# Scores one item ahead, two-headed maps, all convolution taps on VectorE, and x tiles squared first

## What is computed

```python
def layer(x, mod, p, lam, rope, cache):            # per layer, context and latent tokens
    h = rms(x, norm1_g) * (1 + sc1) + sh1
    u = h @ w_in                                     # 1024 -> 2048, split among four mixers
    qa, ka, va, pool_in, glu_in, qd, kd, vd = split(u)
    o_a = softmax(rope(rms(qa)) @ rope(rms(ka)).T / 8) @ va       # 4 query heads, 2 key heads of 64
    o_b = multiscale_pool(pool_in)                   # windows 2, 4, 8, 16
    c = depthwise_conv(a * sigmoid(gate), conv_dw_w) + conv_dw_b  # 256 channels, 31 taps
    o_c = silu(layer_norm(c)) @ conv_pw_w
    # differential attention, 4 heads: q and k split into halves of 32
    P = softmax(q1 @ k1.T) - lam * softmax(q2 @ k2.T)
    o_d = rms(P @ vd, diff_subln_g) * (1 - lambda_init)
    x = x + g1 * concat(o_a, o_b, o_c, o_d) @ w_out
    h2 = rms(x, norm2_g) * (1 + sc2) + sh2
    return x + g2 * expert_choice_ffn(h2)            # 16 experts, SwiGLU, top-k tokens of each
```

## Time and profile before

| what | value |
|---|---|
| median of 3 runs | 2134.52 us (2133.85 to 2135.9) |
| profiled execution, its own time | 2133.39 us |
| its span, first to last instruction | 2131.6 us |
| TensorE clock granted, mean of the span | 0.93 of full |
| busy: PE, DVE, ACT, POOL | 1845.3, 591.4, 470.8, 449.6 us |
| phase 1, layer 0: x stage (to the first projection matmul), projections | to 59.4, to 232.8 us |
| phase 2, layer 0 | 232.8 to 396.9 us |
| experts, layer 0 (536 to 1068 us) | PE busy 525.6 of 532 us, DMA at 388 GB/s |
| phase 1, layer 1: first projection matmul | 1102.0 us |
| phase 2, layer 1: start | 1278.1 us |

### The profile page before, as it was taken

One profiled execution on the slowest core, in us unless ns is written; L12 is line 12 of the kernel. 1 busy time (PEld: TensorE's weight loads), 2 busy tenths in 40 slices (PEclk: granted clock), 3 DMA queues, 4 the chain that ended last, 5 costly groups with the idle time before them and its releaser, 6 DMA issues.

```text
span 2131.6 us, 38834 instructions
## 1 busy us (share of the span) xinstructions
PE 1845.3 (87%) x16748; PEld 920.7 (43%) x16748; DVE 591.4 (28%) x1035; ACT 470.8 (22%) x1208; POOL 449.6 (21%) x410
## 2 busy tenths in 40 slices
PE   3998677895999999999959878879849999999994
PEld 2554455452344444444435435544424444444442
DVE  1365455234011010110126644542331101101011
ACT  2100255111221221221220014441112212212122
POOL 0155233100111111111113642330001111111112
PEclk8999799896999999999969988999879999999997
DMA  9220700327799999999950125004339999999996
GB/s 384 88 79 0 300 36 1 139 89 279 278 401 394 395 401 395 394 402 395 401 219 1 79 98 238 1 1 178 148 108 381 402 394 395 401 394 402 394 394 240
DMA packets 146546, 539.16 MB, mean 253 GB/s; under 512 B 8304, under 2 KB 14544, under 8 KB 146480
## 3 DMA queue, kind: packets, MB, share of 16 engines
q1 hardware_dynamic: 118512, 468.88, 55.3%
q10 hardware_dynamic: 14400, 43.41, 5.4%
q0 software_dynamic: 13568, 25.96, 5.1%
HBM read 511.71 MB, written 26.64 MB: 253 GB/s over the span
## 4 chain that ended last, share of the span: by engine, by line
PE 66%; DMA 18%; DVE 5%; ACT 3%; issue 3%; SPq 1%; POOL 1%; POOLq 1%; ACTq 0%; DVEq 0%
PE PS L794 22%; DMA ring<-in_exp_w_up 15%; PE PS L802 11%; PE PS L723 7%; PE PS L527 4%; PE PS L486 4%; PE PS L487 3%; PE PS L586 2%; PE PS L488 2%; PE PS L425 2%; PE PS L666 2%; DMA ring<-in_w_mod 1%; PE PS L593 1%; SPq L369 1%; PE PS L639 1%
## 5 line engine op out<-in xcount | busy, mean ns | idle before, releaser
L794 PE MATMUL PS<-ring,arena 128*32 128x512 f32 x6144 | 684.6, 596 | 17.8 <-ACT gate_rows L902 9.2
L794 PEld LDWEIGHTS PS<-ring,arena 128*32 128x32 f32 x6144 | 202.0, 110 | 439.7 <-issue 406.5
L802 PE MATMUL PS<-ring,arena 128*32 128x256 f32 x6144 | 349.5, 379 | 0.0
L802 PEld LDWEIGHTS PS<-ring,arena 128*32 128x32 f32 x6144 | 205.5, 110 | 166.9 <-issue 56.7
L1694 POOL DMA_INDIRECT x_rows<-arena x64 | 102.2, 1597 | 652.8 <-DVE arena L1501 602.8
L1115 ACT ACTIVATE arena<-PS,modB,modA 128x64 f32<-128x64 f32 x272 | 84.0, 413 | 395.6 <-PE PS L781 395.6
L723 PE MATMUL PS<-ring,H 128*128 128x512 f32 x320 | 142.7, 606 | 1.2 <-DVEq L1173 1.2
L1680 POOL DMA_INDIRECT arena<-xn_rows,arena x68 | 68.0, 1000 | 343.2 <-DVE arena L1487 253.8
L1275 DVE SCALAR_TENSOR_TENSOR arena<-arena,par 128x655 f32<-128x655 f32 x106 | 121.9, 1150 | 3.5
L486 PE MATMUL PS<-ring,H 128*128 128x512 f32 x160 | 87.3, 629 | 22.1 <-DVE mod L1183 19.0
L1324 DVE TENSOR_REDUCE stat<-PS 128x2 f32<-128x1280 f32 (+1 forms) x60 | 76.6, 1277 | 107.4 <-PE PS L593 98.0
(11 more groups left out here) (209 smaller groups left out, 1937.7 us busy)
## 6 DMA issues: line engine op xcount, KB each, us to landing
ring<-in_exp_w_gate SPq DMA_DIRECT2D x64, 2048.0 KB, 17.8
ring<-in_exp_w_up SPq DMA_DIRECT2D x64, 2048.0 KB
ring<-in_exp_w_down SPq DMA_DIRECT2D x64, 2048.0 KB
ring<-in_w_mod SPq DMA_DIRECT2D x18, 2048.0 KB, 7.7
ring<-in_w_in SPq DMA_DIRECT2D x8, 2048.0 KB, 25.7
arena<-in_w_mod ACTq DMA_DIRECT2D x6, 2048.0 KB, 14.5
ring<-in_w_out SPq DMA_DIRECT2D x4, 2048.0 KB
arena<-x_rows ACTq DMA_DIRECT2D x15, 512.0 KB, 7.3
```

The costliest lines, as they stand in the source:

```text
L794: last = mm(PS[64 * c + r:64 * c + r + LANE, bank, :], left[:, c0 + r:c0 + r + LANE], ring[:, s0 + k // 4, k % 4, c * HALF:(c + 1) * HALF] ...
L802: last = mm(PS[32 * j:32 * j + 32, bank, 0:QUART], left[:, c0:c0 + 32], ring[:, s0 + k // 4, k % 4, j * QUART:(j + 1) * QUART], start=(k = ...
```

## The change

1. **Order on TensorE in the attention.** The body of the loop becomes `item(l, k)`. Item 0 comes first; then item k+1 is given out ahead of the pieces of item k.
2. **Order on ScalarE.** An item's exponentials come ahead of its pieces.
3. **Differential pairs.** A pair is now (c, part): for the two heads of chunk c the map of part 0 or of part 1. The scores are two matmuls of 512 columns on separate row groups and one of 256 for the cached keys (their host-side packing `spread` follows). The first pair of a unit isn't scaled, GpSimd scales the second (two instructions), and VectorE does both subtractions when the second pair is two back. gqa maps are scaled by two instructions instead of one.
4. **Taps.** All 62 are on VectorE: 18 after f(1), 31 after f(3), then 3, 3, 3, 4. GpSimd's taps, its buffer and the addition in item "mean" go; the last tap announces `c_y`.
5. **x stage.** ScalarE squares all five tiles before anything else, and VectorE normalises all five before its first evacuation. TensorE turns x(0) and x(1), does the first half of j(0), turns x(2) to x(4), does the second half of j(0), then f(0) to f(5). j(0) waits for the evacuation of tile 0 alone, f(0) for that of all.

```diff
-        PAIRS = (("gqa", 0), ("diff", 0), ("diff", 1), ("gqa", 1), ("diff", 2), ("diff", 3))
+        PAIRS = (("gqa", 0, 0), ("diff", 0, 0), ("diff", 0, 1), ("gqa", 1, 0), ("diff", 1, 0), ("diff", 1, 1))
...
+        def scaled(n):
+
+            return 4 * (n // 6) + (1, 1, 2, 3, 3, 4)[n % 6]
+
         def maps_of(v):
 
             t, kind, c, last = unit(v)
             bufs = probs if t < LT else probs_ctx
-            if kind == "gqa":
-                return [(bufs[last % 6], i * (TOK if t < LT else P)) for i in range(2)]
-            return [(bufs[(last - 1) % 6], 0), (bufs[last % 6], 0)]
+            buf = bufs[(last if kind == "gqa" else last - 1) % 6]
+            return [(buf, i * (TOK if t < LT else P)) for i in range(2)]
...
                     b0 = 2 + 3 * (t % 2)
                     if ks[0] == 0:
-                        pe.wait_ge(b0_evac, 10 * l + NT)
-                        pe.wait_ge(b1_evac, 10 * l + NT)
+                        pe.wait_ge(b0_evac, 10 * l + 1)
+                        pe.wait_ge(b1_evac, 10 * l + 1)
...
+                        if i == 0:
+                            pe.wait_ge(b0_evac, 10 * l + NT)
+                            pe.wait_ge(b1_evac, 10 * l + NT)
...
-                for t in range(NT):
+                step_x(l, 0)
+                step_x(l, 1)
+                step_j(l, 0, range(0, 4))
+                for t in range(2, NT):
                     step_x(l, t)
-                for ks in (range(0, 4), range(4, KD)):
-                    step_j(l, 0, ks)
-                    step_f(l, 0, ks)
-                for i in range(1, 6):
+                step_j(l, 0, range(4, KD))
+                for i in range(6):
...
-                    kind, i = PAIRS[r]
+                    kind, c, part = PAIRS[r]
                     area = set_at(k)
+                    qc, kc = (c, 2) if kind == "gqa" else (3 + c, 5 + c)
                     for m in range(2):
-                        if kind == "gqa":
-                            rows, qc, kc = slice(64 * m, 64 * m + 64), i, 2
+                        r0 = 64 * m + 32 * part
+                        rows = slice(r0, r0 + (64 if kind == "gqa" else 32))
+                        lhs = qkT[rows, qc, t * P:(t + 1) * P]
+                        if t < LT:
+                            mm(area[:, 1024 * m:1024 * m + LAT], lhs, qkT[rows, kc, 0:LAT], start=True, stop=True)
                         else:
-                            r0 = 32 * (2 * (i % 2) + m)
-                            rows, qc, kc = slice(r0, r0 + 32), 3 + i // 2, 5 + i // 2
-                        lhs = qkT[rows, qc, t * P:(t + 1) * P]
-                        if t == LT:
                             last = mm(area[:, 896 * m:896 * m + P], lhs, qkT[rows, kc, LAT:TOK], start=True, stop=True)
-                        elif m == 0:
-                            mm(area[:, P:512], lhs, qkT[rows, kc, 0:LAT - P], start=True, stop=True)
-                            left, right = lhs, qkT[rows, kc, LAT - P:LAT]
-                        else:
-                            mm(area[:, 1024:1536], lhs, qkT[rows, kc, 0:LAT], start=True, stop=True)
                     if t < LT:
-                        mm(area[:, 512:640], left, right, start=True, stop=True)
-                        for m in range(2):
-                            last = mm(area[:, 896 * m:896 * m + P], qkT[:, i if kind == "gqa" else 3 + i // 2,
-                                                                        t * P:(t + 1) * P],
-                                      kcS[:, 0 if kind == "gqa" else 1 + i, m * P:(m + 1) * P], start=True, stop=True)
+                        both = area[:, 512:1024].rearrange("p (a n) -> p a n", a=4)[:, 0:4:3, :]
+                        last = mm(both, qkT[:, qc, t * P:(t + 1) * P],
+                                  kcS[:, 0 if kind == "gqa" else 1 + 2 * c + part, :].rearrange("p (m n) -> p m n", m=2),
+                                  start=True, stop=True)
                     last.then_inc(t_scores, 1)
...
-                for k, (kind, x) in enumerate(ITEMS):
+                def item(l, k):
+                    kind, x = ITEMS[k]
...
+                item(l, 0)
+                for k in range(len(ITEMS)):
+                    if k + 1 < len(ITEMS):
+                        item(l, k + 1)
                     for v, piece in PIECES[k]:
...
+                for t in range(NT):
+                    squares(l, t)
...
-                squares(l, 0)
                 for t in range(NT):
-                    if t + 1 < NT:
-                        squares(l, t + 1)
...
-                    for v, which in PIECES[k]:
-                        piece(l, v, which)
                     if kind == "p":
                         exponentials(l, k, x)
...
+                    for v, which in PIECES[k]:
+                        piece(l, v, which)
...
+                    if (i, k) == (1, TAPS - 1):
+                        done.then_inc(c_y, 1)
+                    else:
+                        link(done)
+
+                taps = [(0, k) for k in range(TAPS)] + [(1, k) for k in range(TAPS)]
...
-                normalise(l, 0)
+                for t in range(NT):
+                    normalise(l, t)
...
-                conv_taps(16)
+                conv_taps(18)
                 step_f(l, 3)
-                conv_taps(20)
+                conv_taps(31)
...
-                    conv_taps(5 if t < LT else 4)
+                    conv_taps(3 if t < LT else 4)
...
-                    if PAIRS[r][0] == "gqa":
+                    if PAIRS[r][2] == 0:
                         return
                     w = TOK if t < LT else P
-                    out = (probs if t < LT else probs_ctx)[r]
+                    out = (probs if t < LT else probs_ctx)[r - 1]
+                    other = (probs if t < LT else probs_ctx)[r]
                     dve.wait_ge(t_rec, NP * l + n + 1)
-                    dve.wait_ge(p_scaled, NP * l + n + 1)
-                    V.scalar_tensor_tensor(out[:, 0:w], out[:, 0:w], stat[:, 80 + 2 * (n % 4):81 + 2 * (n % 4)],
-                                           out[:, w:2 * w], ALU.mult, ALU.add).then_inc(p_hat, 1)
+                    dve.wait_ge(p_scaled, NU * l + scaled(n))
+                    for m in range(2):
+                        c = 80 + 2 * ((n - 1) % 4) + m
+                        V.scalar_tensor_tensor(out[:, m * w:(m + 1) * w], out[:, m * w:(m + 1) * w], stat[:, c:c + 1],
+                                               other[:, m * w:(m + 1) * w], ALU.mult, ALU.add).then_inc(p_hat, 1)
...
-                        dve.wait_ge(c_part, l + 1)
-                        V.tensor_tensor(y3[:, 1, :], y3[:, 1, :], wb[:, 0:OUTW], ALU.add).then_inc(c_y, 1)
...
-                def conv_tap(k):
-                    if k == DVE_TAPS:
-                        return G.tensor_scalar(wb[:, 0:OUTW], u[:, 1, k:k + OUTW], cwT[:, 1, k:k + 1], None, ALU.mult)
-                    link(G.tensor_scalar(tap, u[:, 1, k:k + OUTW], cwT[:, 1, k:k + 1], None, ALU.mult))
-                    return G.tensor_tensor(wb[:, 0:OUTW], wb[:, 0:OUTW], tap, ALU.add)
...
+                        if PAIRS[r][0] == "diff" and PAIRS[r][2] == 0:
+                            continue
                         reach(t_rec, NP * l + x + 1)
-                        if PAIRS[r][0] == "gqa":
-                            both = out[:, 0:2 * w].rearrange("p (m n) -> p m n", m=2)
-                            G.tensor_tensor(both, both, rec.unsqueeze(2).to_broadcast([P, 2, w]),
-                                            ALU.mult).then_inc(p_scaled, 1)
-                        else:
-                            G.tensor_scalar(out[:, w:2 * w], out[:, w:2 * w], rec[:, 1:2], lams[:, 5:6],
-                                            ALU.mult, ALU.mult).then_inc(p_scaled, 1)
+                        for m in range(2):
+                            half_ = out[:, m * w:(m + 1) * w]
+                            if PAIRS[r][0] == "gqa":
+                                last = G.tensor_scalar(half_, half_, rec[:, m:m + 1], None, ALU.mult)
+                            else:
+                                last = G.tensor_scalar(half_, half_, rec[:, m:m + 1], lams[:, 5:6], ALU.mult, ALU.mult)
+                        last.then_inc(p_scaled, 1)
...
-                spread[l, r0:r0 + 32, 1 + h, m] = ckT[r0:r0 + 32, 1 + h // 2]
+                spread[l, r0:r0 + 32, 1 + 2 * (h // 2) + m, h % 2] = ckT[r0:r0 + 32, 1 + h // 2]
```

27 lines of the change are left out of this document (9 added, 18 removed).

## The result

| | before | after |
|---|---|---|
| median | 2134.18 us (4 runs) | 2205.81 us (4 runs, 2202.4 to 2211.5) |
| ratio | 1 | 1.0338 (95% interval 1.0313 to 1.0363) |
| span of the profiled execution | 2131.6 us | 2202.1 us |
| granted clock, mean | 0.930 | 0.913 |

A forecast was written before the change was run, and what follows sets the result against it. No engine was taken as full in the attention; a loop of waits sets the time. 2133.4 - 9.7 - 0.95 - 3.2 - 3.05 + 1.0 = 2117.5, with 1.1 for the median 2118.5 us; 8-in-10 range 2098 to 2132.

The forecast's parts named there:

- Untouched: Experts and output projections: not touched by the change, filled by DMA and TensorE, so no gain comes from them.
- Clock, +3: Steady attention: one more fall of TensorE's clock, lasting two thirds of a group, costs 3 us in each layer.
- Part 1: Layer 0's x stage: first projection matmul at 46.0 instead of 59.42, net -9.7 us, bounds -7 and -11.
- Part 2: Layer 1's x stage: late x tiles, j(0) 4.7 us earlier, 3.7 coming back, net -0.95 us.
- Parts 3 and 4: Taps all on VectorE, -1.6 us a layer; GpSimd's drain at layer 1's phase end no longer delays TensorE, -3.05 us.
- VectorE's cover: VectorE's idle time before its statistics for j(1): shrinks from 11.3 to about 4 us, still hiding the added taps.
- rival C: Middle taps late on VectorE, TensorE waiting at j(1) and j(2): +5.4 us a layer, 2129 us; chance 0.13.
- Part 5: Attention, +0.5 us a layer: start -2.8, steady part +4.8, clock +3, tail -4.5.
- walk along the loop: Steady attention's loop of waits over three pairs, summed step by step: 14.8 us a group against 14.2 before.
- rival B: TensorE's clock low through much of the steady attention: +29 us a layer, worst case 2176, times above 2134; chance 0.13.
- A: Attention: clock stays up and loop doesn't lengthen, -7.3 us a layer, 2103 us; chance 0.22.
- D: Layer 0's x stage gives -3 instead of -9.7 and layer 1's drain stays: 2128 us; no chance of its own.

The follow-up runs named there:

- x_only: The kernel before with the change's x stage alone, taps and attention as before: 2123.7 us, ratio 0.9944.
- xt: The kernel before with the change's x stage and taps, attention as before: 2114.7 us, ratio 0.9908.
- a_free: The changed kernel with 66 idle semaphore increments on TensorE at the program's start and 63 at layer 1's start, moving the code: 2144.9 us, ratio 1.0053.
- a_fill: a_free with the first four value chunks of every gqa unit made three times on TensorE: 2138.8 us, ratio 1.0019.
- a_pad: The changed kernel with 65 idle semaphore increments on TensorE ahead of layer 0's expert loop and 62 ahead of layer 1's: 2171.4 us, ratio 1.0185.
- a_pad257: The changed kernel with 257 idle semaphore increments on TensorE ahead of layer 0's expert loop alone: 2245.7 us, ratio 1.0535.
- b_pad: The kernel before with 66 idle semaphore increments on TensorE ahead of layer 0's expert loop: 2203.8 us, ratio 1.0333.

## Why the prediction was wrong

I forecast 2118.5 us and measured 2205.8. Of my sum, four of five parts held (one beyond its bounds), one term was mis-sized, and one cause had no step at all. "Untouched", said of the experts, and "Clock, +3", said of the attention, are the two steps that failed.

**Part 1, x stage of layer 0: right.** j(0) at 46.0 forecast, 46.68 measured; net -9.7 forecast, -9.2 measured (130.50 to 121.31).

**Part 2, x stage of layer 1: right.** -0.95 forecast. In x_only the experts up to the first projection are 561.5 us and not 565.9 (-4.4), and the phase behind it 179.5 and not 176.1 (+3.4): -1.0.

**Parts 3 and 4, taps and drain: right in direction, too small.** Forecast -1.6 in layer 0 with a bound of -2.2; xt against x_only has -3.5, and no run says where the rest comes from. Forecast -1.6 and -3.05 in layer 1; measured 179.5 to 174.2, -5.3. Part 4 came true by the earlier end that it names ("some 8 us earlier"); its condition, that the drain is long for GpSimd's last operations, didn't hold: the drain is as good as the same length without them. VectorE's cover held, and rival C didn't occur.

**Part 5, attention: the clock term failed.** I split a_free's layer 1 by VectorE's copies of units to H. Up to the third it is 2.3 us shorter (forecast -2.8). The twelve after it, the steady part, take 99.3 us and not 81.0: +18.2 where I had +4.8 and +3. The rest is 3.2 us shorter (forecast -4.5). The walk along the loop itself was good: 14.8 us a group forecast (its terms, added again, make 14.9), 14.97 measured where the clock stayed high (a_fill). What failed was "Clock, +3": taking the walk's +4.8 off leaves 13.4 us. I priced one more fall for the whole stretch, although my own walk had a fixed order in which TensorE waits for ScalarE in every group. Here the clock fell in each of them, for over 6 us of the 17, and the four inner groups lost 2.5 us each on average, 2.1 of it to the clock (17.05 - 14.97); the first and the last group lost 4.2 and 4.0, the last at a granted clock of 0.55 over its 15 us. That is rival B, which I gave 0.13. Its place was right, and its sign too (a granted clock of 0.80, under 0.85). Its price of 4.8 us a group was for a clock that is low all through; it was low for 0.4 of the time and cost 2.1.

What I argued against rival B was that "in this loop it waits in pieces already and keeps 0.97". The longest of those pieces was 1.4 us, as the view of TensorE's waits over before's steady stretch has it (in total, times, longest):

```profile
PE PS L639 <- DVE H L1352: 5.3, 6, 0.9
PE PS L586 <- ACT H L1016: 3.8, 3, 1.3
PE PS L666 <- DVE arena L1349: 3.7, 6, 0.7
PE PS L586 <- ACT arena L1016: 2.9, 2, 1.4
```

The new one is up to 2.3 us and comes six times in six groups (11.4 us in all, 263.5 to 366 us); a single other wait for ScalarE there is 2.5. I had not asked how long TensorE's longest wait of a group would be. The order had it: ScalarE's fifth copy stands behind a maximum of 1.50 and the exponentials, and TensorE has nothing else queued before that last chunk.

By the Trainium skill (TensorE: Matmul & The Clock Gate, HAM oscillation — how this bites in real kernels), waits between groups of matmuls can throttle the clock anew in every turn of a loop. I had set that against the 0.97 of the trace of before and sided with the trace; the trace of after agrees with the page, with 0.80 over three groups and a stretch of 0.50 in each.

**The missing step: where the code lies.** 58 of the 71 us came from the experts of layer 0, which I had called untouched and put at nothing. The change makes TensorE's program shorter (5 score matmuls of a pair became 3, less 191 instructions up to the loop), and that moved the loop by a quarter of a block of 256 instructions. a_pad, a_pad257, b_pad and a_free show it from both sides. What I read from them: the loop of 1604 instructions is 6.27 blocks long. Beginning in the first three quarters of a block it lies in seven blocks, else in eight. The only place at which it was refetched is 145 (modulo 256, from an unknown origin); 18, 80 to 83 and 209 to 211 were harmless. The eight-block places fill 67 of 256 positions, and such a stretch fits between 83 and 209, so this reading agrees with all twelve loops of the table; where exactly it begins and ends was not tried, and that it is the count of blocks is argued, not shown. In the changed kernel the instruction queue in one whole turn, 605 to 680 us, is this, and the six turns behind it have nine packets each too:

```profile
q8 instruction: 9, 0.15, 0.8%
```

So the whole loop is fetched again each time, not a missing block alone, and one packet more than the eight blocks that I count. What it costs is 58 us in all: 5.92 us of standing and 3.5 us of low clock behind it at a return, seven times, less what the next loads made up.

The Trainium skill (Runtime: NRT & Kernel Launch, Instruction fetch mechanics) gives TensorE a first-in first-out instruction memory of 128 KiB, 2048 instructions, refilled in blocks of 16 KiB, 256 instructions. My estimate from these figures: a loop in eight blocks just fills it, and the block fetched ahead, behind the loop's end, drives out the first. The packets of 16 KB, nine to a turn, and the two kinds of places agree with it; no run here shows the size of the memory itself.

I had this in hand before the result: the changed program has 4241 TensorE instructions ahead of layer 0's loop where there were 4432, and before's trace has its instruction packets. I read neither for the stage that carries a loop.

**The rivals.** A (clock up, no longer loop) is out by 14.97 and by the clock. C and D didn't occur. One smaller slip: half of 1.98 is 0.99 and not 1.04, which would make part 1 -9.8. The sum with the causes put in: 2118.5 + 56.8 (refetching: the experts' stage +52.4, of which the x stage's -4.4 is in the sum already) + 29.9 (attentions +17.2 and +12.7) - 1.0 (what I had for them) - 2.1 (the larger gains of parts 3 and 4, less 0.5 in part 1) + 2.7 (router stages and layer 1's experts, not explained) = 2204.8, beside 2205.8 measured.

## What to carry to other kernels

When a change alters the number of instructions ahead of a hardware loop, look at the loop too: count the instruction packets in its stretch, before and after. If they recur with every turn, shift the code where the engine waits anyway (a few dozen instructions at the program's start cost nothing here and gave back the 58 us). When an order is turned round inside a loop, walk the loop for the longest single wait of TensorE, not only for the sum: price a wait that recurs in each turn with the matmuls behind it at the low clock, as a rival at least. And test the parts of a bundled change apart: x stage and taps alone made 2114.7 us, 0.9% better than before, and were buried under the rest.
